# Low-query score products on 64 rows of the array, attention heads written out, and loads moved in two later stages

## The chip, the cores and the metric

The kernel runs on one core of a Trainium2 chip. The metric is device time in microseconds (us). Every number of the profile is from one profiled execution of the kernel before.

## What is computed

One layer of an encoder on 2048 positions of width 1024, all in float32, and a final norm:

```
u = rms_norm(x); [q|k|v|b|c|h] = u @ w_in
s = q_block @ k.T + bias            # 4 heads, 2 parts each, 64 wide
p = softmax(s);  a = p[part 0] - lam * p[part 1]
att = rms_norm(a @ v) * 0.8
conv = b * conv3(c * h)
x = x + concat(att, conv) @ w_out
z = rms_norm(x)
x = x + (silu(z @ w_gate) * (z @ w_up)) @ w_down
out = rms_norm(x)
```

## The kernel before

All operands of the large products are split into a high part and a low part (float32r), and a product is the sum of high x high, high x low and low x high. The program is five instruction streams, one for each engine, with semaphores between them; the order of each stream is written out by hand.

**Projection.** TensorE turns u and multiplies by w_in (L1523). Queries and keys go to DRAM in both parts (projected_t and projected_qk_lo_t). At the very start L1515 runs four small products with 32 rows, and L1532 transposes u with 128.

**Attention.** 64 query tiles of 128 rows: 16 per head, 4 heads. A tile has four score units, `score_unit` (L1574 to L1585): one of the two parts and one half of the keys (1024). A unit writes two banks of 512 columns in PSUM. The key tile k_sum holds the high keys in partitions 0 to 63 and the low keys in 64 to 127 (`load_k`, L436), and the query tiles hold the same 64 rows twice (`load_q`, L428). So a matmul of 128 rows with q_part_hi gives high x (high + low), and a second with q_part_lo gives low x (high + low): two for each bank, four for a unit. VectorE adds the bias and takes the maximum (L1204), which frees the unit's banks; ScalarE takes exponentials (L827); POOL scales and adds the two parts (L680, L683). TensorE transposes the result by groups of four (`turn_group`, L1599), ScalarE and VectorE split it (L837, L1219), and TensorE multiplies by the values (`value_part`, L1606). PE_ORDER, ACT_ORDER and DVE_ORDER give each stream's order for the four kinds of step (t % 4).

Each stream runs `attention_step` for 8 tiles written out (PROLOGUE), then a hardware loop over three heads whose body is 16 steps (LATER, steps 8 to 23), and 16 steps written out for the last head. The loops are at L496 (SP), L690 (POOL), L879 (ScalarE), L1262 (VectorE) and L1657 (TensorE). So tiles 24 and 40 stand right behind a jump back, and tile 56, the same kind of step, stands in written-out code.

**Out.** 16 row tiles. For tile n, TensorE multiplies the split mixed tile m_part by w_out (`project_tile`, L1675), VectorE adds the rows (L1289), ScalarE takes the square sum (L903), POOL the root (L701), and VectorE makes z_tile (L1295), which TensorE transposes in `turn_z` (L1685) behind the next projection. On ScalarE (L961 to L971) and VectorE (L1401 to L1417) the split of m for tile n + 2 stands between adding the rows of tile n and making its z_tile. SP feeds this with one queue (L548 to L569): load_m (L505, into m_raw, two slots), store_z (L525), store_rows (L520), load_rows (L513).

**Gate and up.** The positions are worked in two halves; each has 22 steps of seven block products (L1710) on the blocks of a Strassen-like scheme. The z blocks of a half stay in seven slots. During the last step of the first half, each slot is refilled: SP loads a block into a staging tile (`load_z_next`, L577; two tiles, z_stage), ScalarE makes its high part (L917) and VectorE its low part (L1300), both behind the matching weight split (L932, L1340). The order of SP is:

```
gate_up_step(0, F_CHUNKS - 3, F_CHUNKS - 3, 1, F_CHUNKS - 1)
load_z_next(0)
gate_up_step(0, F_CHUNKS - 2, F_CHUNKS - 2, 0, 0)
load_z_next(1)
sp.wait_ge(w_lo_ready_2, 7 * F_CHUNKS)
load_gate_up(1, 1)
for k in range(2, 5):
    load_z_next(k)
store_hid(0, F_CHUNKS - 1, F_CHUNKS - 1, 0)
load_z_next(5)
load_z_next(6)
store_hid(0, F_CHUNKS - 1, F_CHUNKS - 1, 1)
```

ScalarE's copy of the first product, L936, comes once in each step and marks its beginning. **Down** (L1763) and the final norm follow.

Of the kernel before, what the change touches and what calls it, by code (L numbers as in the profile page):

```python
# [23 lines left out]
P = 128  # L24
BANK = 512
# [20 lines left out]
def build(nc, x, norm_mix_g, w_in, lambda_q1, lambda_k1, lambda_q2, lambda_k2, subln_g, rel_bias, conv_w,  # L46
# [11 lines left out]
    with ExitStack() as kept:  # L58
        def sem(name):
            return kept.enter_context(nc.semaphore(name))  # L60
# [190 lines left out]
        def at(offset, name, shape, dt=FP32):  # L251
            return nc.alloc_sbuf_tensor_at(name, shape, dt, offset=origin + offset)
# [15 lines left out]

        w_at = [81920 + 4096 * k for k in range(3)] + [4096 * k for k in range(4)]
        w_slot = [[at(tail + w_at[k] + 2048 * n, f"w_{'hi' if n == 0 else 'lo'}_{k}", [P, 4, P], F32R) for n in range(2)] for k in range(7)]  # L270
        z_stage = [at(tail + 73728, "z_stage_0", [P, 4, BANK]), at(tail + 28672, "z_stage_1", [P, 4, BANK])]
        p_0 = at(tail + 16384, "p_0", [P, BANK])
        u_2 = at(tail + 18432, "u_2", [P, BANK])
        u_3 = at(tail + 20480, "u_3", [P, BANK])
# [49 lines left out]
            sem, ("o_summed", "rows_added", "row_sumsq_ready", "row_mean_ready", "row_rstd_ready"))  # L324
        z_ready, z_turned_ready, zt_ready, zt_sum_ready = map(sem, ("z_ready", "z_turned_ready", "zt_ready", "zt_sum_ready"))
        z_stored = [sem(f"z_stored_{i}") for i in range(2)]
        z_loaded = [sem(f"z_loaded_{i}") for i in range(2)]
        z_hi_ready, z_lo_ready = sem("z_hi_ready"), sem("z_lo_ready")
        z_placed = [sem(f"z_placed_{k}") for k in (4, 5, 6)]
        gu_loaded = [sem(f"gate_up_loaded_{i}") for i in range(2)]  # L330
# [16 lines left out]
        def _(sp):  # L347
# [87 lines left out]

            def load_k(h, j):  # L436

                for n, src in enumerate((qkv_dram[HEADS:2 * HEADS], qk_lo_dram[HEADS:2 * HEADS])):
                    piece = src[bass.ds(h, 1), :, j * BANK:(j + 1) * BANK].rearrange("o (c r) s -> r (o c) s", c=2)
                    slot = k_sum[n * DH:(n + 1) * DH, bass.ds(h % 2, 1), :, j * BANK:(j + 1) * BANK]  # L440
                    sp.dma_start(slot.rearrange("p o c s -> p (o c) s").bitcast(FP32), piece).then_inc(k_loaded, 16)

            def load_v(h, j):
# [49 lines left out]

            for t in PROLOGUE:
                attention_step(0, t)
            with sp.Fori(0, HEADS - 1) as h:  # L496
                for t in LATER:
                    attention_step(h, t)
            for t in LATER:
# [5 lines left out]
            def load_m(n):  # L505
                if n >= 2:
                    sp.wait_ge(m_lo_ready, n - 1)
                i = ORDER[n]
                for part, src in ((slice(0, 4), att_dram), (slice(4, 8), conv_dram)):
                    sp.dma_start(m_raw[:, n % 2, part], src.rearrange("(kt p) s -> p kt s", p=P)[:, :, i * P:(i + 1) * P]  # L510
                                 ).then_inc(m_loaded[n % 2], 16)
# [34 lines left out]
                                 ).then_inc(gu_loaded[slot], 16)  # L546

            for n in range(N_ROWS):  # L548
                if n + 2 < N_ROWS:
                    load_m(n + 2)  # L550
                if n == 2:
                    load_gate_up(0, 0)
                if n % 2 == 0 and n >= 2:
                    store_z(n // 2 - 1)
                if n == N_ROWS - 1:

                    sp.wait_ge(o_summed, N_ROWS)
                    for k in (4, 5, 6):
                        sp.dma_start(z_slot[k][1][:, :, :].bitcast(FP32), z_dram[0, k].rearrange("k p t -> p k t")).then_inc(z_placed[k - 4], 16)
                store_rows(n)  # L560
                if n + 2 < N_ROWS:
                    load_rows(n + 2)
                if n in (10, 11, 12, 13):

                    if n == 10:
                        sp.wait_ge(z_stored[0], 16 * 28)
                    else:
                        sp.wait_ge(z_lo_ready, n - 10)
                    sp.dma_start(z_stage[0][:, :, :], z_dram[0, n - 10].rearrange("k p t -> p k t")).then_inc(z_loaded[0], 16)  # L569
# [6 lines left out]

            def load_z_next(k):  # L577

                sp.wait_ge(z_lo_ready, 7 + k - 1)
                sp.wait_ge(z_stored[1], 16 * 28)  # L580
                sp.wait_ge(rows_stored[k % 2], 16 * (N_ROWS // 2))
                sp.dma_start(z_stage[k % 2][:, :, :], z_dram[1, k].rearrange("k p t -> p k t")).then_inc(z_loaded[k % 2], 16)

            def gate_up_step(half, step, chunk, slot, next_chunk=None):

# [12 lines left out]
                gate_up_step(0, 2 * pair + 1, 2 * pair + 1, 1, 2 * pair + 3)  # L598
                gate_up_step(0, 2 * pair + 2, 2 * pair + 2, 0, 2 * pair + 4)
            gate_up_step(0, F_CHUNKS - 3, F_CHUNKS - 3, 1, F_CHUNKS - 1)  # L600
            load_z_next(0)
            gate_up_step(0, F_CHUNKS - 2, F_CHUNKS - 2, 0, 0)
            load_z_next(1)
            sp.wait_ge(w_lo_ready_2, 7 * F_CHUNKS)
            load_gate_up(1, 1)
            for k in range(2, 5):
                load_z_next(k)
            store_hid(0, F_CHUNKS - 1, F_CHUNKS - 1, 0)
            load_z_next(5)
            load_z_next(6)  # L610
            store_hid(0, F_CHUNKS - 1, F_CHUNKS - 1, 1)
            with sp.Fori(0, F_CHUNKS // 2 - 1) as pair:
# [48 lines left out]
        def _(pool):  # L661
# [25 lines left out]

            for t in PROLOGUE:
                attention_step(0, t)
            with pool.Fori(0, HEADS - 1) as h:  # L690
                for t in LATER:
                    attention_step(h, t)
            for t in LATER:
# [24 lines left out]
        def _(act):  # L718
# [157 lines left out]
            fill_far(0, 0)  # L876
            for t in PROLOGUE:
                attention_step(0, t)
            with act.Fori(0, HEADS - 1) as h:  # L879
                for t in LATER:  # L880
                    attention_step(h, t)
            for t in LATER:
# [29 lines left out]
            def split_z(half, k, stage, loads):  # L912

                act.wait_ge(z_loaded[stage], 16 * loads)
                if half:
                    act.wait_ge(product_ready, 7 * (F_CHUNKS - 1) + k + 1)
                nc.scalar.activation(z_slot[k][0][:, :, :], z_stage[stage][:, :, :], ACT.Copy).then_inc(z_hi_ready, 1)  # L917
# [29 lines left out]
            def gate_up_step(step, slot, later=None):  # L947
                copy_p_0(step)
                for k in range(7):
                    if k == 2:  # L950
                        silu_first(step)
                    split_w(step + 1, 1 - slot, k)
                    if later:
                        later(k)
                silu_second(step)
# [36 lines left out]
            with act.Fori(0, F_CHUNKS // 2 - 1) as pair:  # L992
                gate_up_step(2 * pair + 1, 1)
                gate_up_step(2 * pair + 2, 0)
            gate_up_step(F_CHUNKS - 1, 1, lambda k: split_z(1, k, k % 2, (5 if k % 2 == 0 else 1) + k // 2))
            with act.Fori(F_CHUNKS // 2, F_CHUNKS - 1) as pair:
                gate_up_step(2 * pair, 0)
                gate_up_step(2 * pair + 1, 1)
# [36 lines left out]
        def _(dve):  # L1035
# [223 lines left out]
            nc.vector.memset(mean_col[:, :], 1.0 / P)  # L1259
            for t in PROLOGUE:  # L1260
                attention_step(0, t)
            with dve.Fori(0, HEADS - 1) as h:  # L1262
                for t in LATER:
                    attention_step(h, t)
            for t in LATER:
# [32 lines left out]
            def split_z(half, k, stage):  # L1298
                dve.wait_ge(z_hi_ready, 7 * half + k + 1)
                nc.vector.tensor_tensor(z_slot[k][1][:, :, :], z_stage[stage][:, :, :], z_slot[k][0][:, :, :].bitcast(FP32),  # L1300
                                        ALU.subtract).then_inc(z_lo_ready, 1)
# [72 lines left out]
            def gate_up_step(step, slot, later=None, next_sums=True):  # L1374

                for k in range(7):
                    if k == 1:
                        make_u_2(step)
                    if k == 3:
                        make_u_3(step)  # L1380
                    if k == 4:
                        make_c_22(step)
                    if k == 5:
                        make_c_21(step)
                        hidden(step, 0)
                    if k == 6:
                        make_c_12(step)
                    split_w(step + 1, 1 - slot, k)
                    if k == 1:
                        sum_weights(step + 1, 1 - slot, 1)  # L1390
                    if later:
                        later(k)
                if next_sums:
                    sum_weights(step + 2, slot, 0)
                hidden(step, 1)
# [49 lines left out]
            with dve.Fori(0, F_CHUNKS // 2 - 1) as pair:  # L1445
                gate_up_step(2 * pair + 1, 1)
                gate_up_step(2 * pair + 2, 0)
            gate_up_step(F_CHUNKS - 1, 1, lambda k: split_z(1, k, k % 2))
            with dve.Fori(F_CHUNKS // 2, F_CHUNKS - 1) as pair:
                gate_up_step(2 * pair, 0)  # L1450
                gate_up_step(2 * pair + 1, 1)
# [59 lines left out]
        def _(pe):  # L1511
# [62 lines left out]
            def score_unit(h, t, unit):  # L1574


                part, half = divmod(unit, 2)
                pe.wait_ge(bias_added, 64 * h + 4 * t + unit + 1)
                for n in range(2):
                    for b in range(2):  # L1580
                        last = nc.tensor.matmul(scores[:, unit % 2, b * BANK:(b + 1) * BANK],  # L1581
                                                q_part[n][:, (t // 4) % 2, part, t % 4 * P:(t % 4 + 1) * P],
                                                k_sum[:, bass.ds((h + t // 16) % 2, 1), part, half * HALF + b * BANK:half * HALF + (b + 1) * BANK],
                                                start=(n == 0), stop=(n == 1))
                last.then_inc(scores_ready, 1)  # L1585

# [67 lines left out]
            pe.wait_ge(conv_evacuated, 4 + 12 * CONV_GROUPS)  # L1654
            for t in PROLOGUE:
                attention_step(0, t)
            with pe.Fori(0, HEADS - 1) as h:  # L1657
                for t in LATER:
                    attention_step(h, t)
            for t in LATER:  # L1660
# [149 lines left out]
```

## Time and profile before

| | us |
|---|---|
| median of 3 runs | 2845.05 (2843.8 to 2846.85) |
| the profiled execution | 2845.61 |
| its span | 2843.8 |
| mean granted TensorE clock | 0.976 |
| attention | about 574 to 1232 |
| out | about 1232 to 1500 |
| gate and up | about 1500 to 2341 |
| down and final norm | about 2341 to the end |

PE is TensorE's matmuls and PEld its weight loads, DVE is VectorE, ACT is ScalarE, POOL is GpSimd, SPq is SyncE's queue of DMA issues. A matmul's recorded length is longer than the time for which it keeps the next one from starting; the pace is read from start to start. In rows of the order of time, the first number is the start, the second the length of the merged instructions, xN their number, and brackets give the idle time ahead and what ended it.

### The profile page before, as it was taken

Reading aid. Unit: us, or ns where it says so; the run is one execution under the profiler, and the core shown is the slowest. Engines: PE = TensorE matmul, PEld = TensorE weight load, DVE = VectorE, ACT = ScalarE, POOL = GpSimd, SP = SyncE. Lnnn points to the kernel's source line nnn. Section 1 sums busy time; section 2 is a strip of 40 time slices with the busy share of each in tenths; the row PEclk is TensorE's granted clock in tenths of the full one; section 3 lists DMA queues with packets and bytes.
Section 4 is the critical chain, followed back from the end, with each engine's and each line's share of the span. In section 5 each row is a group of like instructions: output and inputs, shape, how many; then the busy total and the mean of one; then the engine's idle time right before and its main releaser. Section 6 shows DMA issues by size and latency. Waiting matters only on the chain. (4 is left out here: it accounts for less than half of the span.)

```text
span 2843.8 us, 36364 instructions
## 1 busy us (share of the span) xinstructions
PE 2679.2 (94%) x12280; PEld 2198.5 (77%) x12280; DVE 1537.0 (54%) x2651; ACT 1026.3 (36%) x1435; POOL 487.3 (17%) x279
## 2 busy tenths in 40 slices
PE   7999999979999899979889999989999999999997
PEld 5788888857777777767668888867888878888886
DVE  5311133268878788834356666666666653434343
ACT  4210000057767676622233333333333322323232
POOL 1000000057767676700000000000000000000000
PEclk9999999999999999979989999999999999999999
DMA  5542111223121311046573222243222225556463
GB/s 166 148 125 81 52 37 38 65 55 74 45 64 36 73 44 45 8 141 190 191 246 93 83 85 89 74 156 95 74 84 86 86 70 180 174 173 203 145 203 117
DMA packets 257354, 298.15 MB, mean 105 GB/s; under 512 B 15200, under 2 KB 175456, under 8 KB 257280
## 3 DMA queue, kind: packets, MB, share of 16 engines
q1 hardware_dynamic: 254400, 287.83, 34.4%
q0 software_dynamic: 2304, 8.39, 0.7%
q10 hardware_dynamic: 576, 1.05, 0.1%
q8 instruction: 34, 0.56, 0.1%
q14 instruction: 40, 0.33, 0.0%
HBM read 212.28 MB, written 84.93 MB: 105 GB/s over the span
## 5 line engine op out<-in xcount | busy, mean ns | idle before, releaser
L1710 PE MATMUL banks<-z_hi,w_hi 128*128 128x512 f32 x1204 | 470.9, 391 | 17.1 <-ACT p L936 9.5
L1710 PE MATMUL banks<-z_lo,w_hi 128*128 128x512 f32 x1204 | 470.5, 391 | 0.0
L1710 PE MATMUL banks<-z_hi,w_lo 128*128 128x512 f32 x1204 | 470.3, 391 | 0.0
L1204 DVE CUSTOM_DVE_ANT_0 exp<-scores,window 128x1024 f32<-128x1024 f32 x256 | 310.2, 1220 | 48.8 <-issue 48.8
L1523 PE MATMUL projected<-u_t_hi,w_part_hi 128*128 128x512 f32 (+1 forms) x768 | 300.9, 392 | 5.3 <-DVE u_t_lo L1068 2.6
L1523 PE MATMUL projected<-u_t_lo,w_part_hi 128*128 128x512 f32 (+1 forms) x768 | 300.0, 391 | 0.0
L1523 PE MATMUL projected<-u_t_hi,w_part_lo 128*128 128x512 f32 (+1 forms) x768 | 299.8, 390 | 0.0
L683 POOL TENSOR_TENSOR exp<-exp,exp 128x2048 f32<-128x2048 f32 x64 | 295.3, 4614 | 5.3
L1710 PEld LDWEIGHTS banks<-z_hi,w_hi 128*128 128x128 f32 x1204 | 227.4, 189 | 65.3 <-DVE w_lo L1340 9.9
L827 ACT ACTIVATE exp<-exp,neg_max 128x2048 f32<-128x2048 f32 x128 | 256.8, 2006 | 38.6 <-DVE neg_max L1210 38.2
L1710 PEld LDWEIGHTS banks<-z_lo,w_hi 128*128 128x128 f32 x1204 | 227.4, 189 | 47.3
L1710 PEld LDWEIGHTS banks<-z_hi,w_lo 128*128 128x128 f32 x1204 | 227.3, 189 | 47.2
L711 POOL TENSOR_TENSOR y_rstd<-y_mean,neg_half 128x1 f32<-128x1 f32 x16 | 8.7, 544 | 1344.6 <-DVE y_mean L1473 1344.6
L932 ACT ACTIVATE w_hi<-w_sum 128x512 fp32r<-128x512 f32 x176 | 111.2, 632 | 313.9 <-PE banks L1710 307.6
L1763 PE MATMUL banks<-down_hi,hid_hi 128*128 128x512 f32 x704 | 218.1, 391 | 4.2 <-DVE down_lo L1461 4.2
L1763 PE MATMUL banks<-down_lo,hid_hi 128*128 128x512 f32 x704 | 217.6, 390 | 0.0
L1763 PE MATMUL banks<-down_hi,hid_lo 128*128 128x512 f32 x704 | 217.6, 390 | 0.0
L1581 PE MATMUL scores<-k_sum,q_part_hi 128*128 (+1 forms) x512 | 178.2, 430 | 30.4 <-DVE row_max L1204 30.2
L837 ACT ACTIVATE a_t_hi<-tile_turned 128x512 fp32r<-128x512 f32 x256 | 147.9, 596 | 143.7 <-PE tile_turned L1599 143.2
L1458 DVE TENSOR_TENSOR hid_lo<-hid_raw,hid_hi 128x512 fp32r<-128x512 f32 x88 | 60.9, 692 | 247.0 <-ACT hid_hi L1007 247.0
L1219 DVE TENSOR_TENSOR a_t_lo<-tile_turned,a_t_hi 128x512 fp32r<-128x512 f32 x256 | 173.0, 688 | 34.5 <-ACT a_t_hi L837 32.3
L1523 PEld LDWEIGHTS projected<-u_t_hi,w_part_hi 128*128 128x128 f32 x768 | 144.8, 189 | 36.3 <-issue 4.4
(145 smaller groups left out, 4231.0 us busy)
## 6 DMA issues: line engine op xcount, KB each, us to landing
down_raw<-in_w_down SPq DMA_DIRECT2D x88, 512.0 KB, 4.4
gate_raw<-in_w_gate SPq DMA_DIRECT2D x44, 512.0 KB, 4.8
up_raw<-in_w_up SPq DMA_DIRECT2D x44, 512.0 KB, 6.0
hidden_t<-hid_stage SPq DMA_DIRECT2D x88, 256.0 KB, 2.6
hid_raw<-hidden_t SPq DMA_DIRECT2D x88, 256.0 KB, 3.7
w_raw<-in_w_in SPq DMA_DIRECT2D x24, 512.0 KB, 5.5
projected_t<-stage SPq DMA_DIRECT2D x48, 256.0 KB, 2.6
z_stage<-z_blocks SPq DMA_DIRECT2D x11, 1024.0 KB, 6.0
```

The lines of the kernel that those rows point to most:

```text
L683: nc.gpsimd.tensor_tensor(exp_0[:, slot_0], exp_0[:, slot_0], exp_1[:, slot_1], ALU.add).then_inc(mixed_ready, 1)
L711: nc.gpsimd.tensor_tensor(y_rstd[:, n:n + 1], y_mean[:, n:n + 1], neg_half[:, 0:1], ALU.pow).then_inc(y_rstd_ready, 1)
L827: nc.scalar.activation(rows, rows, ACT.Exp, bias=neg_max[:, t % 2, part:part + 1], accum_out=exp_sum[:, part, t % 16:t % 16 + 1]).then_inc ...
L837: nc.scalar.activation(dst, turned_bank(h, t, index), ACT.Copy).then_inc(group_hi, 1)
L932: nc.scalar.activation(w_slot[k][0][:, :, :], src, ACT.Copy).then_inc(w_hi_ready_2, 1)
L1204: nc.vector.tensor_tensor_reduce(out=rows[:, half * HALF:(half + 1) * HALF], in0=scores[:, unit % 2], in1=window[:, window_slice(t, half)] ...
L1219: nc.vector.tensor_tensor(parts[1][at], turned_bank(h, t, index), parts[0][at].bitcast(FP32), ALU.subtract).then_inc(group_lo, 1)
L1458: nc.vector.tensor_tensor(hid_part[slot][1][:, :], hid_raw[:, slot], hid_part[slot][0][:, :].bitcast(FP32), ALU.subtract).then_inc(f_lo_re ...
L1523: last = nc.tensor.matmul(projected[:, bank * BANK:(bank + 1) * BANK], w_part[w][:, r, kt], u_t[u][:, kt, rows], start=(kt == 0 and n == 0 ...
L1581: last = nc.tensor.matmul(scores[:, unit % 2, b * BANK:(b + 1) * BANK], q_part[n][:, (t // 4) % 2, part, t % 4 * P:(t % 4 + 1) * P], k_sum ...
L1710: last = nc.tensor.matmul(c_bank[BANK_OF[k]], w_slot[k][w][:, kt], z_slot[k][z][:, kt], start=(kt == 0 and t == 0 and k in (0, 1, 3, 4)), ...
L1763: last = nc.tensor.matmul(y_banks[j][:, c * BANK:(c + 1) * BANK], hid_part[slot][h][:, j * P:(j + 1) * P], down_part[slot][w][:, c * BANK: ...
```

## The change

It does five things. The second pair of matmuls of a score unit (low queries) now uses 64 rows of the array each: bank 0 rows 0 to 63 and bank 1 rows 64 to 127, against the high keys alone. For that, load_k puts the high keys of odd 512-column pieces into partitions 64 to 127 and the low keys into 0 to 63. The product low x low is thereby left out. The loop over heads becomes Python code, written out, in all five streams. In out, both loads of m of a pair are issued at the even tile, ahead of the pair's stores. z_stage gets a third tile, at an offset that zt_sum used, with its own semaphore, and the refill's order on SP changes.

```
-        z_stage = [at(tail + 73728, "z_stage_0", [P, 4, BANK]), at(tail + 28672, "z_stage_1", [P, 4, BANK])]
+        z_stage = [at(tail + offset, f"z_stage_{i}", [P, 4, BANK]) for i, offset in enumerate((73728, 28672, 49152))]
...
             def load_k(h, j):
...
-                    slot = k_sum[n * DH:(n + 1) * DH, bass.ds(h % 2, 1), :, j * BANK:(j + 1) * BANK]
+                    at = (n + j) % 2 * DH
+                    slot = k_sum[at:at + DH, bass.ds(h % 2, 1), :, j * BANK:(j + 1) * BANK]
...
-            with sp.Fori(0, HEADS - 1) as h:
+            for h in range(HEADS - 1):
                 for t in LATER:
                     attention_step(h, t)
...
             for n in range(N_ROWS):
-                if n + 2 < N_ROWS:
+
+                if n % 2 == 0 and n + 2 < N_ROWS:
                     load_m(n + 2)
+                    load_m(n + 3)
...
             def load_z_next(k):
-                sp.wait_ge(z_lo_ready, 7 + k - 1)
+                sp.wait_ge(z_lo_ready, 7 + k - 2)
...
-                sp.dma_start(z_stage[k % 2][:, :, :], z_dram[1, k].rearrange("k p t -> p k t")).then_inc(z_loaded[k % 2], 16)
+                sp.dma_start(z_stage[k % 3][:, :, :], z_dram[1, k].rearrange("k p t -> p k t")).then_inc(z_loaded[k % 3], 16)
...
-            load_z_next(0)
+            for k in range(3):
+                load_z_next(k)
             gate_up_step(0, F_CHUNKS - 2, F_CHUNKS - 2, 0, 0)
-            load_z_next(1)
             sp.wait_ge(w_lo_ready_2, 7 * F_CHUNKS)
             load_gate_up(1, 1)
-            for k in range(2, 5):
+            for k in range(3, 6):
                 load_z_next(k)
             store_hid(0, F_CHUNKS - 1, F_CHUNKS - 1, 0)
-            load_z_next(5)
             load_z_next(6)
...
                 pe.wait_ge(bias_added, 64 * h + 4 * t + unit + 1)
-                for n in range(2):
+                for n, rows in ((0, (slice(0, P), slice(0, P))), (1, (slice(0, DH), slice(DH, P)))):
                     for b in range(2):
                         last = nc.tensor.matmul(scores[:, unit % 2, b * BANK:(b + 1) * BANK],
-                                                q_part[n][:, (t // 4) % 2, part, t % 4 * P:(t % 4 + 1) * P],
-                                                k_sum[:, bass.ds((h + t // 16) % 2, 1), part, half * HALF + b * BANK:half * HALF + (b + 1) * BANK],
+                                                q_part[n][rows[b], (t // 4) % 2, part, t % 4 * P:(t % 4 + 1) * P],
+                                                k_sum[rows[b], bass.ds((h + t // 16) % 2, 1), part, half * HALF + b * BANK:half * HALF + (b + 1) * BANK],
                                                 start=(n == 0), stop=(n == 1))
```

The same replacement of Fori by range is made in the streams of POOL, ScalarE, VectorE and TensorE, and split_z of ScalarE and VectorE takes its stage by k % 3.

## Rows read from the trace of the kernel before

**Rows 1.** The page: busy time of each engine.

```profile
PE 2679.2 (94%) x12280; PEld 2198.5 (77%) x12280; DVE 1537.0 (54%) x2651; ACT 1026.3 (36%) x1435; POOL 487.3 (17%) x279
```

**Rows 2.** Stretch out: us; busy PE, PEld, DVE, ACT, POOL; clock; DMA; GB/s.

```profile
1232.00:1500.00 268.00, 224.83 (x988) 183.91 (x989) 120.08 (x135) 80.05 (x95) 9.45 (x17) 0.91 0.64 207
```

**Rows 3.** TensorE's waits in the whole span: us in total, times, longest.

```profile
PE scores L1581 <- DVE row_max L1204: 30.2, 34, 4.8
PE banks L1685 <- DVE z_tile L1295: 25.6, 6, 9.8
...
PE banks L1710 <- ACT p L936: 9.5, 1, 9.5
...
PE banks L1710 <- DVE u L1346: 7.6, 1, 7.6
```

**Rows 4.** TensorE in order of time: start of a score unit, what follows it, transposes.

```profile
901.47 0.62 PE L1581 MATMUL scores<-k_sum,q_part_hi 128*128 x2
...
902.39 0.39 PE L1606 MATMUL o_sum<-a_t_hi,v_part_hi 128*128 128x512 f32 x1
...
805.26 1.03 PE L1599 MATMUL tile_turned<-identity,exp 128*128 128x128 f32 x8
```

**Rows 5.** TensorE around 15 us, 32 rows to 128 (two windows); L1515's group, ns.

```profile
13.20 1.91 PE L1515 MATMUL projected<-onehot,rel_wide 32*128 32x512 f32 x2
15.04 0.69 PE L1532 MATMUL u_turned<-identity,u_tile 128*128 128x128 f32 x2
...
15.30 0.63 PE L1532 MATMUL u_turned<-identity,u_tile 128*128 128x128 f32 x2
...
L1515 PE MATMUL projected<-onehot,rel_wide x8: 1056/1056/1215, 7.9 to 14.1; 32*128 32x512 f32 x8
```

**Rows 6.** Busy time by stretch, columns as in rows 2: four query tiles, 28 to 31.

```profile
850.40:888.20 37.80, 36.19 (x200) 29.46 (x198) 31.98 (x84) 26.92 (x39) 28.09 (x13) 1.00 0.21 52
```

**Rows 7.** The same for tiles 23, 24 (at a jump back), 55 and 56.

```profile
798.70:812.10 13.40, 10.36 (x60) 8.45 (x58) 8.56 (x23) 9.60 (x15) 6.78 (x3) 0.99 0.40 94
812.10:820.90 8.80, 7.41 (x30) 6.26 (x31) 7.79 (x21) 3.80 (x5) 6.71 (x3) 0.63 0.92 194
1119.50:1129.00 9.50, 9.50 (x54) 7.94 (x53) 8.52 (x24) 6.75 (x10) 6.77 (x3) 1.00 0.16 45
1129.00:1136.60 7.60, 6.92 (x40) 5.11 (x38) 7.53 (x23) 6.48 (x11) 5.91 (x3) 1.00 0.58 120
```

**Rows 8.** VectorE in order of time at the jump back.

```profile
812.06 0.06 DVE L1203 MEMSET wait_pad<- 128x1 f32 x1 [3.85 <-issue]
```

**Rows 9.** ScalarE's waits between 1228 and 1500.

```profile
ACT m_part_hi L893 <- DMA m_raw<-projected_t: 76.1, 12, 12.3
```

**Rows 10.** Order of time in out: SP's issues, then TensorE.

```profile
1308.47 2.25 SPq L510 DMA_DIRECT2D m_raw<-projected_t  x1
...
1325.93 0.43 SPq L510 DMA_DIRECT2D m_raw<-att_t  x1
...
1335.64 1.97 PE L1685 MATMUL banks<-identity,z_tile 128*128 128x128 f32 x8 [4.27 <-DVE z_tile L1295]
```

**Rows 11.** ScalarE in order of time: starts of the half's last step and the next.

```profile
1883.74 0.60 ACT L936 ACTIVATE p<-banks 128x512 f32<-128x512 f32 x1 [1.36 <-PE banks L1710]
...
1924.61 0.58 ACT L936 ACTIVATE p<-banks 128x512 f32<-128x512 f32 x1
```

**Rows 12.** z_stage: ScalarE's late split, SP's issues, VectorE's group (ns), landing.

```profile
1919.20 1.91 ACT L917 ACTIVATE z_hi<-z_stage 128x2048 fp32r<-128x2048 f32 x1 [9.56 <-DMA z_stage<-z_blocks]
...
1913.32 0.98 SPq L582 DMA_DIRECT2D z_stage<-z_blocks  x2
...
L1300 DVE TENSOR_TENSOR z_lo<-z_stage,z_hi x11: 2283/2292/2294, 1422.2 to 1924.6; 128x2048 fp32r<-128x2048 f32 x11
...
DMA to landing us min/median/max: 5.6/6.0/8.2
```

**Rows 13.** Busy time by stretch: undisturbed steps of gate and up.

```profile
1942.00:2320.00 378.00, 378.00 (x1670) 313.09 (x1669) 237.09 (x357) 120.00 (x199) 0.00 (x0) 1.00 0.27 80
```

More of the change, by code:

```diff
@@ L326, in build @@
         z_stored = [sem(f"z_stored_{i}") for i in range(2)]
-        z_loaded = [sem(f"z_loaded_{i}") for i in range(2)]
+        z_loaded = [sem(f"z_loaded_{i}") for i in range(3)]
         z_hi_ready, z_lo_ready = sem("z_hi_ready"), sem("z_lo_ready")
@@ L689, in _ @@
                 attention_step(0, t)
-            with pool.Fori(0, HEADS - 1) as h:
+            for h in range(HEADS - 1):
                 for t in LATER:
@@ L878, in _ @@
                 attention_step(0, t)
-            with act.Fori(0, HEADS - 1) as h:
+            for h in range(HEADS - 1):
                 for t in LATER:
@@ L994, in _ @@
                 gate_up_step(2 * pair + 2, 0)
-            gate_up_step(F_CHUNKS - 1, 1, lambda k: split_z(1, k, k % 2, (5 if k % 2 == 0 else 1) + k // 2))
+            gate_up_step(F_CHUNKS - 1, 1, lambda k: split_z(1, k, k % 3, (5, 1, 1)[k % 3] + k // 3))
             with act.Fori(F_CHUNKS // 2, F_CHUNKS - 1) as pair:
@@ L1261, in _ @@
                 attention_step(0, t)
-            with dve.Fori(0, HEADS - 1) as h:
+            for h in range(HEADS - 1):
                 for t in LATER:
@@ L1447, in _ @@
                 gate_up_step(2 * pair + 2, 0)
-            gate_up_step(F_CHUNKS - 1, 1, lambda k: split_z(1, k, k % 2))
+            gate_up_step(F_CHUNKS - 1, 1, lambda k: split_z(1, k, k % 3))
             with dve.Fori(F_CHUNKS // 2, F_CHUNKS - 1) as pair:
@@ L1656, in _ @@
                 attention_step(0, t)
-            with pe.Fori(0, HEADS - 1) as h:
+            for h in range(HEADS - 1):
                 for t in LATER:
```

## The prediction

> **What bounds the kernel now.** The page's shares come first [rows 1]: TensorE has work in 94% of the span, no other engine in more than 54%. So time can be won only where TensorE streams less or waits. Then the busy time by stage: in out, TensorE's granted clock is 0.91 of full and its busy time 225 of 268 us [rows 2], the worst of all stages. Third, TensorE's waits [rows 3]: 30.2 us on the bias add that frees a score bank, 25.6 us on z_tile in out, and 9.5 and 7.6 us once each in gate and up. The reader should see that the last three are few, long waits at single places.
>
> **Low queries with 64 rows.** A score unit is four 512-column matmuls. One starts at 901.47 and what follows it at 902.39 [rows 4]: it holds TensorE for 0.92 us, 0.23 for each; the 0.39 us beside a matmul is its length, not its price. There are 256 units. The two high-query matmuls stay; the two low-query ones now use rows 0 to 63 and 64 to 127 and write two banks. If they run side by side, a unit loses 0.23 us: 256 x 0.23 = 59 us of TensorE. But the array now changes its row split twice in each unit. One such change is in the trace, from 32 rows to 128 [rows 5]. Two of the old kind take 1.91 us and one lasts 1.06, so they start 0.85 apart, the last at 14.05; the next kind starts at 15.04, 0.99 later, 0.14 above the pace. Its first two start 0.26 apart; the second and third 0.21 (0.63 less the 0.42 that one lasts), 0.05 less. So a change costs 0.19 us, and at half clock: eight such transposes take 1.03 us in attention [rows 4], at most 0.13 each. [...] Two changes are 0.20 a unit, 51 us, and 0.03 us for the second weight load is 8 us. Net 59 - 51 - 8 = **0**. Bounds: changes free, 59 us less of TensorE; changes at 0.19 and no overlap, 256 x 0.38 = 97 us more.
>
> What TensorE gains doesn't all reach the end. Four tiles, 16 units, take 37.8 us, with TensorE busy 36.2 and VectorE 32.0 [rows 6]. A free overlap would take 3.7 us from TensorE and run near VectorE's floor; I let 60% through, 35 us over 64 tiles. An added cost comes through at 90%. The swapped halves of k_sum in odd banks move the same bytes from the same place in SP's queue: nothing.
>
> [...]
>
> **Heads written out.** The loop over heads has three passes, so two jumps back. The tile at the first takes 13.4 us, and the same step written out 9.5 [rows 7]; VectorE idles 3.85 us on nothing but issue there [rows 8]. The tile behind it takes 8.8 against 7.6, at a clock of 0.63 against 1.00 [rows 7]. 3.9 + 1.2 = 5.1 us, twice: **-10**. Bounds -6 (half comes back as waits on VectorE) and -12. SP's and POOL's heads are written out too, covered by the longer streams. [...]
>
> **Loads ahead of stores in out.** A row tile needs 48 x 0.23 = 11.0 us and 8 transposes, 1.03 us at most [rows 4], some 12 us in all. TensorE waits 25.6 us for z_tile [rows 3]. Why z_tile is late: ScalarE waits 76.1 us, 12 times, for m_raw to land [rows 9], and VectorE splits m before it normalises the rows, so each late load delays z_tile. The load for tile 7 goes out at 1325.9, behind the pair's stores and the rows' load, and TensorE then stands 4.27 us until 1335.6 [rows 10]. In the change it goes out beside tile 6's, at about 1309 [rows 10], where its only wait (the split of tile 5) is over: 17 us earlier, more than a tile. The even loads stay where they are, with 0.5 MB more behind them. So most stalls of odd tiles go, and part of the lowered clock: a mean of 0.91 is 0.18 of 268 us, 48 us, at half. I take **-24**: 25.6 of waits and 6 of clock, less 8 that remain at tiles 12 to 15, where z_stage loads stand in between. Bounds -10 and -31. Next late is TensorE itself. Stores move behind two more DMA issues of some 0.5 us each, covered by SP's own waits.
>
> **Three staging tiles.** A step of gate and up is 84 matmuls; at 1670 in 378 us [rows 13], 19.0 us. The step in which the second half's z is split takes 40.9 (1883.74 to 1924.61 [rows 11]): 22 us lost. TensorE waits 7.6 and 9.5 us [rows 3], because ScalarE waits 9.56 us for z_stage, whose load SP issued only at 1913.3 [rows 12], behind the store that waits for the hidden tile. With three tiles, blocks 0 to 2 are loaded a step early and block 5 ahead of that store; only block 6 is behind it. Next late is VectorE: seven splits of 2.29 us [rows 12], 16 us, on top of its usual 11.9 a step (237.1 in 378 us [rows 13]), make 27.9 us in a step of 19.0. Some 9 us are owed, part of it hidden since each block is wanted a step later. Against this, 3 MB now stand ahead of 1 MB of weights in SP's queue: some 18 us at 6.0 us a block [rows 12], about when VectorE wants the weights; up to 3 us. I take 10 us left of 22: **-12**; bounds -5 and -19.
>
> **The sum.** 0 - 10 - 24 - 12 = -46 us against the profiled execution's 2845.61, which is 0.56 above the median of the runs. 2845.6 - 46 - 0.6 = **2799 us**. The small bounds of the last three add to -21, the large ones to -62.
>
> **Rivals.**
> (A, forecast) The changes of row split eat what the overlap gives: 2799, its own range 2782 to 2818. For it, the 0.19 us of [rows 5].
> (B) Overlap with hardly a price: 2799 - 35 = 2764. For it, that the one row is at half clock and between other kinds of instruction; against it, VectorE's 32.0 of 37.8 [rows 6].
> (C) Overlap, at the full 0.19 a change: 256 x (0.38 - 0.23 + 0.03) = 46 us of TensorE, 90% of it 41: 2840, hardly faster than before.
> (D, slower) The low matmuls don't overlap and a change costs 0.19: 97 us, 90% of it 87, over the 46 won elsewhere: 2886. It decides from the point where a unit grows by 0.20 us.
> (E) The moved loads bring half of what I say, another wait standing behind each, with scores unchanged: 2799 + 23 = 2822.
>
> **Chances.** A 0.42, B 0.23, C 0.13, D 0.08, E 0.14. The range takes in A and E, reaches below B's middle, since B's share of the gain let through is a choice, and ends at C's middle: 2756 to 2840. Left out are D, half of C and a part of B, 2 in 10. A measurement of this kernel can tell about 0.2% (5.7 us) from no change. Faster by more: A, B, E and most of C, 0.87; within: the rest of C, 0.05; slower: D, 0.08.
>
> **What would show it.** A unit from start to start near 0.92 us is A, 0.70 B, 1.10 C, 1.30 D; the two 64-row matmuls under 0.1 apart show the overlap, and 0.23 would refute it. No 13.4 us tile at a head's turn; tiles in out some 12 us apart, and m_raw hardly waited for; the long step of gate and up near 29 instead of 40.9 us. The forecast is wrong if units grow past 1.1 us, or if the stalls in out keep their 25 us.

## The result and the profile after

The changed kernel takes 2826.16 us (median of 4 runs, 2822.77 to 2829.45) against 2845.11 before: a ratio of 0.9933, 95% interval 0.9916 to 0.995. It is 19 us faster, and less than half of the 46 us forecast. Three edits brought about what the prediction said; the fourth, the low-query matmuls on 64 rows, made the kernel slower.

The page of the changed kernel, its span and busy time, and its TensorE's waits (us in total, times, longest). The lines have moved: L1586 was L1581, L1611 was L1606, L1680 was L1675, L1690 was L1685, L1715 was L1710, L896 was L893, L939 was L936.

```profile
span 2821.2 us, 34778 instructions
PE 2699.6 (96%) x12280; PEld 2127.2 (75%) x12280; DVE 1535.2 (54%) x2651; ACT 1024.1 (36%) x1435; POOL 486.8 (17%) x279
...
PE scores L1586 <- DVE row_max L1207: 16.8, 25, 4.4
...
PE banks L1715 <- ACT p L939: 5.5, 1, 5.5
PE banks L1690 <- DVE z_tile L1298: 4.0, 1, 4.0
...
PE banks L1715 <- DVE u L1349: 2.5, 1, 2.5
```

Against [rows 3], the waits for z_tile fell from 25.6 us to 4.0, those at the half's change from 9.5 and 7.6 to 5.5 and 2.5. But TensorE's busy time rose by 20 us from [rows 1] in a span 23 us shorter, with as many matmuls. Something in it has become dearer.

**The score unit.** TensorE of the changed kernel in order of time, one unit between value products, then its weight loads (PEld) there, and the group of the low-query matmuls (ns, shortest/median/longest).

```profile
907.13 0.62 PE L1586 MATMUL scores<-k_sum,q_part_hi 128*128 128x512 f32 x2
907.68 0.50 PE L1586 MATMUL scores<-k_sum,q_part_lo 64*128 64x512 f32 x2
908.11 0.50 PE L1611 MATMUL o_sum<-a_t_hi,v_part_hi 128*128 128x512 f32 x1
908.45 0.39 PE L1611 MATMUL o_sum<-a_t_lo,v_part_hi 128*128 128x512 f32 x1
908.68 0.40 PE L1611 MATMUL o_sum<-a_t_hi,v_part_lo 128*128 128x512 f32 x1
...
907.68 0.18 PEld L1586 LDWEIGHTS scores<-k_sum,q_part_lo 64*128 64x128 f32 x2 [0.36 <-issue]
908.11 0.19 PEld L1611 LDWEIGHTS o_sum<-a_t_hi,v_part_hi 128*128 128x128 f32 x1 [0.25 <-issue]
...
L1586 PE MATMUL scores<-k_sum,q_part_lo x512: 491/493/794, 574.1 to 1212.4; 64*128 64x512 f32 x171
```

Read the starts. Two high-query matmuls and the way to the next take 0.55 us instead of 0.46: the first change of split costs 0.09. Two low-query matmuls then last 0.50 us together, where each of them lasts 0.49 by itself: they do run side by side. Yet the next instruction starts only 0.43 us after them, not 0.23, so 0.20 more; and the one behind it 0.34 later instead of 0.23, so 0.11 more. The two changes cost 0.09 + 0.20 + 0.11 = 0.40 us and the overlap gives 0.23. A unit with what it delays is dearer by 0.17 us. The weight loads say where: each first load behind a change starts together with its matmul, after 0.36 and 0.25 us in which the loader waits for nothing but issue, while the load for the value product at 908.68 starts at 908.45, with the matmul ahead of its own.

Behind 131 of the 256 units stand transposes, and there less is lost. A unit with four transposes up to the next matmul, before, then changed:

```profile
908.22 0.71 PE L1581 MATMUL scores<-k_sum,q_part_hi 128*128 x2
...
909.59 0.47 PE L1606 MATMUL o_sum<-a_t_hi,v_part_hi 128*128 128x512 f32 x1
...
925.41 0.71 PE L1586 MATMUL scores<-k_sum,q_part_hi 128*128 128x512 f32 x2
...
926.89 0.70 PE L1586 MATMUL scores<-k_sum,q_part_hi 128*128 128x512 f32 x2
```

1.37 us became 1.48. An estimate of what TensorE has more to do is 125 x 0.17 + 131 x 0.11 = 36 us.

**The other edits.** Busy time by stretch in the changed kernel (columns as in [rows 2]): tiles 28 to 31, the tile at the former jump back, and the one behind it.

```profile
854.80:893.80 39.00, 37.91 (x197) 25.33 (x196) 31.80 (x83) 26.71 (x39) 28.04 (x13) 1.00 0.22 52
806.50:816.30 9.80, 9.80 (x52) 6.40 (x51) 8.39 (x24) 6.54 (x10) 6.75 (x3) 1.00 0.16 44
816.30:823.90 7.60, 7.28 (x42) 4.51 (x40) 7.53 (x23) 6.51 (x11) 5.91 (x3) 1.00 0.88 196
```

The loss at the jump is gone: 9.8 and 7.6 us where [rows 7] have 13.4 and 8.8. But four tiles take 39.0 instead of 37.8 us [rows 6].

Out in the changed kernel, in order of time: TensorE's first and sixteenth row tile, SP's issues for tiles 8 and 9, ScalarE's wait for m_raw in the stage (us, times, longest).

```profile
1259.53 1.19 PE L1680 MATMUL banks<-o_part_hi,m_part_hi 128*128 128x512 f32 x2 [12.55 <-DVE o_part_lo L1286]
...
1444.51 0.47 PE L1680 MATMUL banks<-o_part_hi,m_part_hi 128*128 128x512 f32 x1
...
1339.08 0.43 SPq L512 DMA_DIRECT2D m_raw<-att_t  x1
1339.56 0.51 SPq L512 DMA_DIRECT2D m_raw<-projected_t  x1
1340.11 0.51 SPq L512 DMA_DIRECT2D m_raw<-att_t  x1
1340.66 0.51 SPq L512 DMA_DIRECT2D m_raw<-projected_t  x1
...
ACT m_part_hi L896 <- DMA m_raw<-projected_t: 17.0, 3, 11.5
```

Both tiles' loads stand together, m_raw is waited for 17.0 us instead of 76.1 [rows 9], and the sixteen tiles start within 185.0 us. Before they took 212.4, from 1247.37, TensorE's first start in out, to 1459.72. Some is given back: from the sixteenth tile to the second copy of p (ScalarE's mark of the next step) it was 43.2 us, now 1444.51 to 1492.18, 47.7. The net is 23 us.

The half's change in the changed kernel: the long step's two marks on ScalarE, its wait for block 6, and SP's issue of that block.

```profile
1872.98 0.60 ACT L939 ACTIVATE p<-banks 128x512 f32<-128x512 f32 x1 [1.36 <-PE banks L1715]
...
1900.62 1.91 ACT L920 ACTIVATE z_hi<-z_stage 128x2048 fp32r<-128x2048 f32 x1 [6.63 <-DMA z_stage<-z_blocks]
...
1902.96 0.58 ACT L939 ACTIVATE p<-banks 128x512 f32<-128x512 f32 x1
...
1894.43 0.37 SPq L586 DMA_DIRECT2D z_stage<-z_blocks  x1
```

The long step takes 30.0 us instead of 40.9 [rows 11]. Part of what is left over is block 6, still behind the store of the hidden tile, as forecast; that ScalarE would stand 6.63 us for it was not.

### The profile page after: what moved, and what is told of

Read it like the earlier page. It is cut to its first block and busy times, and to the rows that moved or that the text cites. A ratio compares the mean times of both kernels' runs of the same rounds, so it can differ in the third digit from the quotient of the medians.

```text
span 2821.2 us, 34778 instructions
## 1 busy us (share of the span) xinstructions
PE 2699.6 (96%) x12280; PEld 2127.2 (75%) x12280; DVE 1535.2 (54%) x2651; ACT 1024.1 (36%) x1435; POOL 486.8 (17%) x279
## 5 line engine op out<-in xcount | busy, mean ns | idle before, releaser
L1715 PE MATMUL banks<-z_hi,w_hi 128*128 128x512 f32 x1204 | 470.0, 390 | 8.4 <-ACT p L939 5.5
L1715 PE MATMUL banks<-z_hi,w_lo 128*128 128x512 f32 x1204 | 469.3, 390 | 0.0
L1715 PE MATMUL banks<-z_lo,w_hi 128*128 128x512 f32 x1204 | 469.3, 390 | 0.0
L1715 PEld LDWEIGHTS banks<-z_hi,w_hi 128*128 128x128 f32 x1204 | 226.8, 188 | 56.5 <-issue 5.9
L1715 PEld LDWEIGHTS banks<-z_lo,w_hi 128*128 128x128 f32 x1204 | 226.8, 188 | 47.2
L1715 PEld LDWEIGHTS banks<-z_hi,w_lo 128*128 128x128 f32 x1204 | 226.5, 188 | 47.4
L1586 PE MATMUL scores<-k_sum,q_part_hi 128*128 128x512 f32 x512 | 184.5, 442 | 17.0 <-DVE row_max L1207 16.8
L1010 ACT ACTIVATE hid_hi<-hid_raw 128x512 fp32r<-128x512 f32 x88 | 55.5, 631 | 324.1 <-PE banks L1768 324.1
```

Of the source, the lines that this page charges most:

```text
L1010: nc.scalar.activation(hid_part[slot][0][:, :], hid_raw[:, slot], ACT.Copy).then_inc(f_hi_ready, 1)
L1715: last = nc.tensor.matmul(c_bank[BANK_OF[k]], w_slot[k][w][:, kt], z_slot[k][z][:, kt], start=(kt == 0 and t == 0 and k in (0, 1, 3, 4)), ...
```

## The experiments

Two theories on why 46 us became 19. Theory 1: the 64-row matmuls lose about 22 us, the other edits bring what was said. Rival: the edits overlap, or the written-out heads lengthen attention. Each edit was first put alone into the kernel before. The 64-row form was tried only on top of the written-out heads, so its own effect is e2 against e1.

**e1, heads alone.** The edit: `with sp.Fori(0, HEADS - 1) as h:` becomes `for h in range(HEADS - 1):` in all five streams.

> The kernel before with the heads written out in all five streams and nothing else. Theory 1 (each jump back costs one 13.4 us tile and a slow one behind it): 10 us less than before, 2835, with tiles 24 and 40 at 9.4 to 9.8 us and the tiles behind them at 7.6. Rival (other waits take the place of the jumps, so writing out gives little, and the 12.9 us by which attention grew in the changed kernel are partly its work): 2842 to 2848, with some other tiles longer than before.

Measured: 2834.82 us against 2847.61 before on the same chip, ratio 0.9956 (0.9944 to 0.9969). The written-out heads gain; they are not what lengthens attention. The two tiles at the first former jump take 9.4 and 7.6 us.

**e2, heads and 64 rows.** e1 with the diff of `load_k` and `score_unit` shown ahead.

> The kernel before with the heads written out and the low-query matmuls on 64 rows (the product low x low is left out); out and gate/up as before. Theory 1 (a unit grows from 0.91 to 0.98 us because the two changes of row split cost 0.10 and 0.19 us and the overlap gives back 0.23): 22 us slower than the kernel with the heads alone, so about 2857 if that one is at 2835, and slower than before. Rival (the unit's growth is not what lengthens attention; the written-out heads are): about the time of the kernel with the heads alone, within 5 us.

Measured: 2858.34 us, ratio 1.0043 (1.0029 to 1.0057): slower than before, and 23.5 us slower than e1. The profiled executions lie 23.9 us apart in their spans, and TensorE's first start in out tells that 22.3 of it have come up by the end of attention. First e1, then e2:

```profile
1237.23 1.19 PE L1675 MATMUL banks<-o_part_hi,m_part_hi 128*128 128x512 f32 x2 [12.70 <-DVE o_part_lo L1283]
```

```profile
1259.50 0.76 PE L1676 MATMUL banks<-o_part_hi,m_part_hi 128*128 128x512 f32 x1 [12.65 <-DVE o_part_lo L1284]
```

**e3, out alone.** The edit to `load_m`'s order, nothing else.

> The kernel before with only both loads of m of a pair issued at the even tile, ahead of the stores. Theory 1: 24 us less than before, 2821; sixteen row tiles from first to last start in 185 us instead of 212, and 3 us given back in the first steps of gate and up. Rival (most of the gain in out in the changed kernel came from the earlier end of attention or another clock, or is given back later): 2830 to 2840.

Measured: 2820.63 us, ratio 0.9907 (0.9892 to 0.9921), 27 us less. Its sixteen tiles start within 184.7 us (1246.04 to 1430.70). This edit alone is worth more than the whole change.

**e4, staging alone.**

> The kernel before with only the third staging tile and its order of loads. Theory 1: 11 to 12 us less than before, 2834; the long step of gate and up takes 30.0 us instead of 40.9, the next 19.9. Rival (the long step depends on how the queue stood before, so alone it gives less): 2838 to 2843.

Measured: 2834.42 us, ratio 0.9954 (0.9941 to 0.9967), 13 us less. ScalarE's marks of the long step, in order of time:

```profile
1887.36 0.60 ACT L935 ACTIVATE p<-banks 128x512 f32<-128x512 f32 x1 [1.36 <-PE banks L1709]
1916.98 0.58 ACT L935 ACTIVATE p<-banks 128x512 f32<-128x512 f32 x1
```

29.6 us. The four parts are -12.8, +23.5, -27.0 and -13.2, together -29.5, where the whole change measured -19. The medians of the kernel before lie up to 3 us apart between chips (2844.76 to 2847.61), and it stands in three of the four parts, so some 7 us of this gap can hang on it alone. Whether the rest is the edits overlapping isn't shown.

**e5, the change without the 64 rows.**

```
-                for n, rows in ((0, (slice(0, P), slice(0, P))), (1, (slice(0, DH), slice(DH, P)))):
+                for n in range(2):
...
-                                                q_part[n][rows[b], (t // 4) % 2, part, t % 4 * P:(t % 4 + 1) * P],
+                                                q_part[n][:, (t // 4) % 2, part, t % 4 * P:(t % 4 + 1) * P],
```

(k_sum likewise, and load_k as before.)

> The changed kernel with its score units as before: four matmuls of 128 rows, the keys laid out as before. Theory 1 (the 64-row matmuls alone lose time, the other three edits add up): 23 us less than the changed kernel, 2795 to 2803, attention in 605 to 607 us from the first tile to the last. Rival (the edits overlap in what they win, so they don't add up): 2808 to 2815.

Measured: 2801.39 us against 2844.76, ratio 0.9843 (0.983 to 0.9857): 43 us less, with three edits that add up to 46 by the forecast. The rival's 2808 to 2815 is missed, but not all of the rival falls: put in alone, the three gave 53 us. Most of the 10 us between can again be the kernel before (2847.61 there, 2844.76 here, counted three times), but an overlap of the edits isn't excluded. The changed kernel takes 25 us more than this one, so the 64-row form costs about the same here (24.8) as in e2 against e1 (23.5).

**e6, block 6 ahead too.** e5 with

```
-            for k in range(3, 6):
+            for k in range(3, 7):
                 load_z_next(k)
             store_hid(0, F_CHUNKS - 1, F_CHUNKS - 1, 0)
-            load_z_next(6)
```

> The same, and the load of z block 6 is issued ahead of the store of the hidden tile too. Theory 1 (the 6.6 us for which ScalarE waits for block 6 hold up its copy of the first product, and through it TensorE by 5.5 us): 5 us less than without this edit, the long step of gate and up at 24 to 25 us instead of 30.0. Rival (VectorE's 27.9 us of work in that step is the bound, not the load): no difference, step at 28 us or more.

Measured: 2793.92 us, ratio 0.9816 (0.9803 to 0.983): 7.5 us less than e5. ScalarE's marks around the long step and its wait for block 6, in order of time:

```profile
1852.37 0.60 ACT L935 ACTIVATE p<-banks 128x512 f32<-128x512 f32 x1 [1.36 <-PE banks L1709]
...
1873.67 1.93 ACT L916 ACTIVATE z_hi<-z_stage 128x2048 fp32r<-128x2048 f32 x1 [0.23 <-DMA z_stage<-z_blocks]
1877.47 0.58 ACT L935 ACTIVATE p<-banks 128x512 f32<-128x512 f32 x1
1894.81 0.60 ACT L935 ACTIVATE p<-banks 128x512 f32<-128x512 f32 x1 [1.36 <-PE banks L1709]
```

The long step takes 25.1 us, and the next 17.3. The two take 42.4 us together, against 49.9 in the changed kernel and 38.0 for two usual ones. VectorE's 27.9 us of work did not hold the step to that length: it is busy for 23.3 of the 25.1 us and for 14.9 of the next 17.3, so a part runs over. What holds the last 4 us isn't shown. This is the fastest complete version, 32 us under the changed kernel.

**e7, the price of a free overlap.** e5 without the low-query matmul of every second bank:

```
                 for n in range(2):
-                    for b in range(2):
+                    for b in range(2 - n):
```

(The stop flag of the second bank moves to its remaining matmul.)

> Score units as before, but the low-query matmul of the second bank is left out, so a unit has three matmuls of 128 rows and no change of row split: what an overlap without a price would give. It leaves out low queries times keys for every second 512 columns. Theory 1 (attention is held by TensorE and VectorE in turn, and about half of a change of TensorE's time comes through, as with the 46 us that the 64-row form adds): 25 to 32 us less than the kernel with all four matmuls. Rival (VectorE's floor stops it): under 15 us less. Second rival (TensorE is the bound throughout): 50 us or more less.

Measured: 2776.4 us, 25 us less than e5, where TensorE has 59 us less to do. Tiles 28 to 31 of e7 (columns as in [rows 2]):

```profile
833.90:869.50 35.60, 33.03 (x178) 25.74 (x176) 31.59 (x85) 26.88 (x39) 28.04 (x13) 1.00 0.22 53
```

37.8 us became 35.6 for 3.7 us less of TensorE, 0.6 in these four; over the whole kernel 25 of 59, 0.42. So the 60% let through in the prediction, read from such tiles, was too high for a gain: rival B would have ended at about 2774, not 2764.

**e8, no overlap.** The changed kernel's units with both low-query matmuls on rows 0 to 63: `(1, (slice(0, DH), slice(0, DH)))`.

> The changed kernel, but both low-query matmuls of a unit use rows 0 to 63, so they can't run side by side, while the array changes its row split as often (keys laid out as before; low x low is left out). Theory 1 (the overlap gives 0.23 us a unit, the changes cost more): the second low matmul starts 0.23 us after the first instead of 0.003, a unit takes 1.20 us instead of 0.98, and the kernel is 35 to 55 us slower than the changed one, 2861 to 2881. Rival (what costs time in the changed kernel is the side-by-side run itself, not the change of split): within 10 us of the changed kernel or faster.

Measured: 2878.95 us, ratio 1.0121 (1.0103 to 1.014), 53 us slower than the changed kernel. TensorE of e8 in order of time, two units behind each other:

```profile
902.61 0.62 PE L1581 MATMUL scores<-k_sum,q_part_hi 128*128 128x512 f32 x2
903.17 0.73 PE L1581 MATMUL scores<-k_sum,q_part_lo 64*128 64x512 f32 x2
903.83 0.73 PE L1581 MATMUL scores<-k_sum,q_part_hi 128*128 128x512 f32 x2
904.49 0.73 PE L1581 MATMUL scores<-k_sum,q_part_lo 64*128 64x512 f32 x2
905.15 0.50 PE L1606 MATMUL o_sum<-a_t_hi,v_part_hi 128*128 128x512 f32 x1
905.49 0.40 PE L1606 MATMUL o_sum<-a_t_lo,v_part_hi 128*128 128x512 f32 x1
```

The pair of low-query matmuls lasts 0.73 instead of 0.50 us: the overlap is worth 0.23, as counted. What stays are the changes: a unit takes 1.22 us (902.61 to 903.83), and 0.34 instead of 0.23 stands behind it, here too. The keys lie as in the kernel before, so the swapped halves of k_sum are not what costs. Of the 256 x 0.23 = 59 us that TensorE has more to do, 53 reach the end, 0.9; tiles 28 to 31 take 41.4 us, and TensorE is busy for all 41.4.

**e9, fewer changes of split.** The changed kernel, with the low-query matmuls first in four of sixteen units:

```
+                products = [(0, (slice(0, P), slice(0, P))), (1, (slice(0, DH), slice(DH, P)))]
+                low_first = (t % 4, unit) in ((0, 1), (0, 3), (1, 1), (2, 3))
+                for n, rows in products[::-1] if low_first else products:
```

> The changed kernel, but in four of sixteen units, those that TensorE takes straight behind another unit, the two low-query matmuls come first, so the array stays on the 64-row split between the two units: 384 changes of split instead of 512, all else alike. Theory 1 (the price goes with the number of changes, 0.41 us for two with their weight loads, and half of TensorE's time comes through): 64 x 0.41 = 26 us less of TensorE, 8 to 14 us less than the changed kernel. Rival (the price is that of the 64-row matmuls themselves, however they are ordered): within 4 us of the changed kernel.

Measured: 2812.11 us (2810.97 to 2812.86), ratio 0.9882 (0.9867 to 0.9897), 14 us less than the changed kernel beside it. TensorE of e9 in order of time, a pair of units:

```profile
834.41 0.62 PE L1584 MATMUL scores<-k_sum,q_part_hi 128*128 128x512 f32 x2
834.96 0.73 PE L1584 MATMUL scores<-k_sum,q_part_lo 64*128 64x512 f32 x4
835.63 0.73 PE L1584 MATMUL scores<-k_sum,q_part_hi 128*128 128x512 f32 x2
836.20 0.39 PE L1609 MATMUL o_sum<-a_t_hi,v_part_hi 128*128 128x512 f32 x1
```

Two units in 1.79 us with nothing left behind, where two of the kernel before take 2 x 0.92 = 1.84. With two changes for two units the overlap just pays here; with two for each it doesn't. The price went with the number of changes, not with the 64-row matmuls. But 384 of the 512 changes are still there, and e9 takes 11 us more than e5, which has no 64-row matmuls.

**e10, the changed kernel again**, beside e9:

> The changed kernel once more, beside the one with low queries first, on the same chip. Theory 1: 2822 to 2830, as before. Rival (its runs differ from chip to chip by as much as the difference sought): outside of that.

Measured: 2826.17 us (2822.19 to 2830.58), ratio 0.9933 (0.992 to 0.9947).

## Why the prediction was wrong

**Low queries with 64 rows: the failed step.** The sum takes 0.10 us for each of a unit's two changes, about half of the 0.19 of [rows 5], and 0.03 us for a second weight load. No run shows either figure: at full clock the two changes cost 0.40, 0.20 each, with all that the weight loads add, which turned the zero of the sum into a loss of 0.17 us a unit. Halving for the clock was a choice that no row backed: the edit's own change costs 0.29 us at half clock (last section), so it falls to two thirds and not to half. The row was of another kind of instruction, too, and low for its clock, 0.19 against 0.29. That it was at half clock is read from the pace alone: L1532's transposes start 0.21 us apart at 15 us and 0.11 at 88.5, where eight take 1.06; the granted clock of the windows is 1.00 in both places. That the same 0.19 left as it was, rival C's figure, comes so near the 0.20 measured at full clock is luck: two errors that cancel. A unit reads 0.98 us from start to start, 1.09 with what it delays, next to the 1.10 named for C.

Runs e8 and e9 show that each change has a price: a unit with both changes and no overlap takes 1.22 us instead of 0.92, and in e9 two units with two changes between them take 1.79, where 1.84 less two overlaps of 0.23 would be 1.38. What the array does in that time they can't tell. The overlap itself loses hardly anything, 0.50 us for two matmuls where one lasts 0.49. So the price of the changes decided, and the sum needed it at full clock.

**How much comes through: mis-sized too.** Rival C had 46 us of TensorE, against some 36 by the estimate above, and took 90% of it to the end, 41 us. It is 23.5 us (e2 against e1), two thirds of 36. The share isn't one number: 0.42 of what e7 takes off TensorE, two thirds of what the 64-row form adds, 0.9 of what e8 adds on top, where TensorE has less left to wait for. It waits 22.3 us for score banks in e5, 16.8 in the changed kernel and 9.8 in e8 (the 30.2 of [rows 3] hold the jumps' share as well, since e1 has 22.3): added work fills waits first. With the share and the work as measured, C would have read 2799 + 24 = 2823, 3 us off.

**Heads written out: right.** -10 forecast; e1 gives -13, and both tiles at the former jump are as said. More code cost nothing that shows: in e1 the instruction queues moved 1.03 MB instead of 0.89, and its tiles of 9.4 and 7.6 us are no longer than 55 and 56 in [rows 7].

**Loads ahead of stores in out: right.** -24 forecast, 23 net in the trace, -27 in e3. The last stall of 4.0 us on z_tile, up to 1429.31, remains in the tiles where the z_stage loads stand in between, as said.

**Three staging tiles: right in size, and one thing under it wrong.** -12 forecast, -13 in e4, which holds the third tile and the new order of loads together. The rest was laid to VectorE's 27.9 us of work; e6 shows that most of it, 7.5 of some 12 us, was ScalarE standing in order for block 6.

**The sum and the rivals.** Without the 64-row edit the same sum gives 2799, and e5 is 2801.4. The match is closer than the runs allow one to say, since the three edits gave 53 us one by one and 43 together. The kernel lies between rival C and rival E; E (moved loads at half) is refuted by e3 and e4, D's missing overlap by the two matmuls in 0.50 us, B by the price. Rival D is what e8 builds: 87 us were said for it, and e8 takes 78 more than e5. What isn't shown is why runs of the changed kernel spread from 2822 to 2831 us.

## What to carry to other kernels

Running two half-height matmuls side by side saved one matmul's 0.23 us for each pair here, but each change between 64 and 128 rows cost 0.20 us. One pair for two changes lost 0.17 us, two pairs for two changes only just gained (1.79 against 1.84 us), so such pairs should stand together; putting the low-query matmuls of neighbouring units next to each other won 14 us back. A cost read from a single row, of another kind of instruction and at another clock, can be wrong in both respects, so its full value belongs in the range. How much of a change in TensorE's work reached the end went with how much it still waited: 0.42 of what was taken off, as its waits for score banks rose from 22.3 us to 27.6, and 0.65 and 0.9 of what was added, as they fell to 16.8 and 9.8. And a bundle should be taken apart: here the kernel with one edit undone and one load moved is 32 us faster than the bundle. Where one queue feeds a chain, look first for a load that stands behind a store which waits: both such edits brought what the rows promised (27 and 13 us by themselves).

## What the runs showed of the hardware

A change of the row split cost TensorE time in two places here: the first matmul on the new split starts about 0.10 us late, together with its weight load, and the one after it another 0.11 late, 0.34 us behind the first instead of 0.23 (changed kernel and e8 alike). It made no difference whether the new split has 64 or 128 rows: in e8 the two matmuls of 128 rows at 903.83 last the same 0.73 us together as the two on rows 0 to 63 at 903.17, where two of 128 rows with no change ahead last 0.62. Where transposes follow the pair of 64 rows, the loss of a unit is 0.06 us smaller, 0.11 instead of 0.17.

At half clock a change cost more, but not twice as much: 0.29 us instead of 0.20. Units of the changed kernel behind each other and their stretch (columns as in [rows 2]), then two matmuls of the kernel before and their stretch at the same clock:

```profile
587.53 1.22 PE L1586 MATMUL scores<-k_sum,q_part_hi 128*128 128x512 f32 x2
588.68 0.79 PE L1586 MATMUL scores<-k_sum,q_part_lo 64*128 64x512 f32 x2
589.40 1.22 PE L1586 MATMUL scores<-k_sum,q_part_hi 128*128 128x512 f32 x2
...
587.53:591.28 3.75, 3.75 (x11) 1.57 (x9) 2.87 (x9) 2.00 (x2) 3.21 (x3) 0.50 0.00 0
...
1903.17 0.63 PE L1710 MATMUL banks<-z_hi,w_lo 128*128 128x512 f32 x1
1903.60 0.63 PE L1710 MATMUL banks<-z_hi,w_hi 128*128 128x512 f32 x1
...
1902.00:1906.00 4.00, 3.84 (x9) 3.07 (x10) 3.88 (x5) 1.31 (x2) 0.00 (x0) 0.50 0.68 257
```

A matmul of 128 rows holds TensorE for 0.43 us at this clock, so four would take 1.72 and the overlap gives 0.43. The unit takes 1.87, and so do the two ahead of it, so its two changes cost 1.87 - 1.72 + 0.43 = 0.58 us, 0.29 each, where they cost 0.40 at full clock.
